# Row trips on ScalarE's DMA queue, a 256-column product placed in front of the first MLP strip, and a warm-up of five wide products in a two-block transformer kernel

## The reference

```python
h = x
a = rms_norm(h, norm_mix[i])
y = stick_breaking_mixer(a, sb_w_qkv[j], sb_w_o[j])
h = h + y
h = h + sq_relu_mlp(rms_norm(h, norm_mlp[i]), mlp_w1[i], mlp_w2[i])
return rms_norm(h, final_norm)
...
h = rms_norm_2(x, pre_mix_g[l])
z = h @ w_in[l]
```

## Time and profile before

| | us |
|---|---|
| median of 3 runs | 2128.96 |
| lowest, highest | 2128.48, 2130.49 |
| the profiled execution | 2131.68 |
| its span in the trace | 2129.9 |
| TensorE busy in it | 2117.4 |

### The profile page before, as it was taken

How to read it: one execution, slowest core, us unless ns; L and a number is a source line. 1 busy time by engine, 2 the same in 40 slices (tenths; PEclk the granted TensorE clock), 3 DMA queues, 4 the chain that set the end, 5 groups by cost and what they waited for, 6 DMA issues and landing times.

```text
span 2129.9 us, 26812 instructions
## 1 busy us (share of the span) xinstructions
PE 2117.4 (99%) x11014; PEld 1816.5 (85%) x11014; DVE 1256.3 (59%) x1337; ACT 1052.1 (49%) x1224; POOL 189.8 (9%) x90
## 2 busy tenths in 40 slices
PE   9999999999999999999999999999999999999998
PEld 8888888888888888888878888888888888888887
DVE  6554656656455554555666755475665644666565
ACT  6554555544334443444545544465555433555543
POOL 3000000000000000000004000002222100222210
PEclk9999999999999999999999999999999999999999
DMA  8565547665666666565675555555555666556663
GB/s 287 173 204 171 184 163 237 227 191 176 207 196 188 190 212 193 176 204 193 223 232 184 175 174 198 190 164 182 181 189 185 216 191 195 173 183 197 207 206 121
DMA packets 218922, 411.97 MB, mean 193 GB/s; under 512 B 13360, under 2 KB 22704, under 8 KB 218288
## 3 DMA queue, kind: packets, MB, share of 16 engines
q1 hardware_dynamic: 217936, 405.77, 59.2%
q10 hardware_dynamic: 864, 4.49, 0.6%
HBM read 403.92 MB, written 6.29 MB: 193 GB/s over the span
## 4 chain that ended last, share of the span: by engine, by line
PE 98%; DVE 0%; DMA 0%; ACT 0%; issue 0%; SPq 0%; POOL 0%; ACTq 0%; DVEq 0%; POOLq 0%
PE ps L1481 98%; DMA passed_rows<-xN 0%; PE ps L1484 0%; ACT Wh L910 0%; DMA E<-passed_rows 0%; DVE Wl L1131 0%; ACT aHL L928 0%; DVE xN L1223 0%; DVE T L1227 0%; SPq L848 0%; ACT T L922 0%; DVE xN L1214 0%; ACT T L1060 0%; DVE QK L1368 0%; ACT raw L1073 0%
## 5 line engine op out<-in xcount | busy, mean ns | idle before, releaser
L1131 DVE TENSOR_TENSOR Wl<-raw,Wh 128x1024 fp32r<-128x1024 f32 x743 | 912.1, 1246 | 649.0 <-ACT Wh L910 648.3
L1481 PE MATMUL ps<-aHL,Wh 128*128 128x512 f32 x3336 | 1162.8, 393 | 2.0 <-DVE aHL L1231 1.5
L910 ACT ACTIVATE Wh<-raw 128x1024 fp32r<-128x1024 f32 x743 | 767.5, 1054 | 587.1 <-PE ps L1481 583.3
L1481 PE MATMUL ps<-aHL,Wl 128*128 128x256 f32 x3328 | 931.9, 280 | 0.0
L1481 PEld LDWEIGHTS ps<-aHL,Wh 128*128 128x128 f32 x3336 | 625.6, 188 | 142.1 <-DVE aHL L1231 1.8
L1481 PEld LDWEIGHTS ps<-aHL,Wl 128*128 128x128 f32 x3328 | 630.6, 189 | 0.6
L1481 PE MATMUL ps<-Wh,hid 128*128 128x512 f32 x1728 | 533.2, 389 | 0.0
L1481 PEld LDWEIGHTS ps<-Wh,hid 128*128 128x128 f32 x1728 | 324.4, 188 | 67.8
L1481 PE MATMUL ps<-Wl,hid 128*128 128x512 f32 x864 | 336.4, 389 | 0.0
L1481 PEld LDWEIGHTS ps<-Wl,hid 128*128 128x128 f32 x864 | 162.2, 188 | 33.1
L1481 PE MATMUL ps<-Wh,oHL 128*128 128x512 f32 x512 | 159.0, 390 | 0.0
(11 more groups left out here) (177 smaller groups left out, 798.1 us busy)
## 6 DMA issues: line engine op xcount, KB each, us to landing
raw<-in_mlp_w_dram SPq DMA_DIRECT2D x256, 512.0 KB, 4.2
raw<-in_w_up_dram SPq DMA_DIRECT2D x176, 512.0 KB, 3.6
raw<-in_sb_w_qkv_dram SPq DMA_DIRECT2D x93, 512.0 KB, 4.7
raw<-in_w_down_dram SPq DMA_DIRECT2D x88, 512.0 KB, 4.0
raw<-in_w_in_dram SPq DMA_DIRECT2D x64, 512.0 KB, 4.3
raw<-in_sb_w_o_dram SPq DMA_DIRECT2D x32, 512.0 KB, 5.1
raw<-in_w_o_dram SPq DMA_DIRECT2D x32, 512.0 KB, 3.7
passed_rows<-xN SPq DMA_DIRECT2D x16, 256.0 KB, 4.3
```

Of the source, the lines that this page charges most:

```text
L910: e.activation(Wh[:, i % NW, :], rawv[:, i % NRAW, :], ACT.Copy).then_inc(st["hi"][0], 1)
L1131: e.tensor_tensor(Wl[:, i % NW, :], rawv[:, i % NRAW, :], Wh[:, i % NW, :].bitcast(F32), ALU.subtract).then_inc(st["lo"][0], 1)
L1481: return e.matmul(o, l, r, start=start, stop=stop, skip_group_check=True)
```

## The change

Three things are changed. The step `move_rows` is split into `pass_rows` and `return_rows`, both in ScalarE's program instead of SP's. The two passes are planned ahead of the squares of the same rows, and the four returns one piece later. The product of ones and `r_a` goes from behind the fifth piece of the first `mlp_w1` strip to in front of its first piece. The ten constant products of 128 columns at the beginning become five of 256.

```diff
--- before.py
+++ after.py
@@ -144,14 +144,11 @@
         st["r3c"], st["r4c"], st["diag"] = first["r"], both, diag
         after(p.at + 2, lambda: spread("r4", "r_b"), ahead=True)
 
-    def wide_product():
-        s = side_set()
-        step("wide_product", set=s, row=st["r1"], free=list(free[f"set{s}"]))
-
     def move_rows(n, gain_name, need):
 
-        moved = done("rows_moved", 4 * 16)
-        step("move_rows", n=n, need=need, free=list(free["E"]), passed=done("rows_passed", 32), done=moved)
+        passed, moved = done("rows_passed", 32), done("rows_moved", 4 * 16)
+        step("pass_rows", n=n, need=need, done=passed)
+        later(1, lambda: step("return_rows", n=n, passed=passed, free=list(free["E"]), done=moved))
 
         def turn_blocks():
             turned = done("blocks_turned")
@@ -270,8 +267,8 @@
             step("add_products", s4=s4, set=s, mm=k, x_rows=x_rows[-1], factor=st["r2sq"] if scaled else None, done=added)
             free[f"set{s}"] = [added[1]]
             if gain_name == "mlp":
+                move_rows(s4, "mlp", added)
                 row_squares(s4, added)
-                move_rows(s4, "mlp", added)
             if gain_name == "pre2":
                 sq = row_squares(s4, added)
 
@@ -279,8 +276,8 @@
                     g = [done("rows_gained") for t in range(2)]
                     step("gain_rows_x", n=s4, need=sq, row=st["final_row"], done=g)
                     st["final_used"] = g[1]
+                    move_rows(s4, "pre2", g)
                     row_squares(s4, g, gained=True)
-                    move_rows(s4, "pre2", g)
                 later(1, gained)
             if more:
                 more(s, k[1])
@@ -321,8 +318,7 @@
             i = strip("mlp_w1", (at + j) * STRIP, ALL8, "aHL", tile_hl, evac_relu(4 * j))
             if at + j == 0:
                 after(i + 3, lambda: row_norm(squared=True))
-                after(i + 4, wide_product)
-            elif j == 0:
+            if j == 0:
                 p.pieces[i]["wide"] = True
         for s4 in range(4):
             i = strip("mlp_w2", s4 * STRIP, tuple(range(2 * at, 2 * (at + n))), "hid1", hid_tiles,
@@ -836,17 +832,6 @@
                 elif k == "load_rows":
                     t, cs = st["c"] // 4, slice(st["c"] % 4 * STRIP, (st["c"] % 4 + 1) * STRIP)
                     e.dma_start(xN[:, t, cs], A["x_rows"][t * 128:(t + 1) * 128, cs]).then_inc(st["done"][0], 16)
-                elif k == "move_rows":
-                    n, cs = st["n"], slice(st["n"] * STRIP, (st["n"] + 1) * STRIP)
-                    for t in range(2):
-                        e.wait_ge(*st["need"][t])
-                        e.dma_start(passed[n, t * 128:(t + 1) * 128, :], xN[:, t, cs]).then_inc(st["passed"][0], 16)
-                    for t in st["free"]:
-                        e.wait_ge(*t)
-                    e.wait_ge(*st["passed"])
-                    for a in range(4):
-                        e.dma_start(moved_rows[a * 32:(a + 1) * 32, :, :],
-                                    passed[n].rearrange("(c j) (a f) -> a j c f", c=8, a=4)[a]).then_inc(st["done"][0], 16)
                 elif k == "load_half":
                     i, t = st["i"], st["t"]
                     w, _, at, col = pieces[i]["src"]
@@ -940,6 +925,18 @@
                     for t in st["need"]:
                         e.wait_ge(*t)
                     e.dma_start(dst, src).then_inc(st["done"][0], 16)
+                elif k == "pass_rows":
+                    cs = slice(st["n"] * STRIP, (st["n"] + 1) * STRIP)
+                    for t in range(2):
+                        e.wait_ge(*st["need"][t])
+                        e.dma_start(passed[st["n"], t * 128:(t + 1) * 128, :], xN[:, t, cs]).then_inc(st["done"][0], 16)
+                elif k == "return_rows":
+                    e.wait_ge(*st["passed"])
+                    for t in st["free"]:
+                        e.wait_ge(*t)
+                    for a in range(4):
+                        e.dma_start(moved_rows[a * 32:(a + 1) * 32, :, :],
+                                    passed[st["n"]].rearrange("(c j) (a f) -> a j c f", c=8, a=4)[a]).then_inc(st["done"][0], 16)
                 elif k == "norm_x":
                     cs = slice(st["q"] * STRIP, (st["q"] + 1) * STRIP)
                     for t in st["need"]:
@@ -1577,8 +1574,9 @@
                                 m.then_inc(p.mm, 1)
                 elif k == "warm_up":
                     e.wait_ge(*st["ones"])
-                    for n in range(10):
-                        mm(ps[0][:, 3, 0:128], ones[:, :], ones[:, :], True, True)
+                    for n in range(5):
+                        mm(ps[0][:, 3, 0:TOK].rearrange("p (t q) -> p t q", t=2), ones[:, :],
+                           ones[:, :].unsqueeze(1).broadcast_to([128, 2, 128]), True, True)
                 elif k == "rms":
                     P = ps[st["set"]]
                     e.wait_ge(*st["need"])
@@ -1600,11 +1598,6 @@
                             mm(ps[st["side"]][:, 0, :], diag, xn[:, 1, cs], False, True).then_inc(st["summed_out"][0], 1)
                 elif k == "turn":
                     turn_tiles(st)
-                elif k == "wide_product":
-                    for t in st["free"]:
-                        e.wait_ge(*t)
-                    e.wait_ge(*st["row"])
-                    mm(ps[st["set"]][:, 1, 0:TOK], ones[:, :], r_a[:, :], True, True)
                 elif k == "spread":
                     e.wait_ge(*st["diag"])
                     for t in st["free"]:
```

## The result

| us | before | after |
|---|---|---|
| median of 20 runs each | 2129.16 | 2133.95 |
| lowest, highest | 2127.54, 2132.55 | 2131.38, 2137.16 |
| the profiled execution | 2131.68 | 2133.41 |

The ratio is 1.0021, 95% interval [1.0015, 1.0027]. The forecast was 2129.3, in a range of 2126.5 to 2132.5: the time lies outside it, on the side to which I had given 0.08.

The account below looks back on a forecast made before the run. TensorE, busy 2117.4 of 2129.9 us, was taken as the bound. From the median 2128.96, -0.26 (product), 0 (warm-up), 0 (seven trips) and +0.6 (eighth trip) made +0.3: 2129.3 us, range 2126.5 to 2132.5.

Parts of the forecast that it names:

- the side to which I had given 0.08: Whole kernel: chance 0.08 that it becomes slower by more than 0.2%, 4.3 us.
- So seven trips cost 0: Trips behind sb_w_o and three of mlp_w2: the weights' lead covers ScalarE's stand, so 0 us.
- The 2.2 us of cover in mlp_w2: Last round of mlp_w2: weights ready at 1079.7 us, wanted at 1081.9, so a trip has 2.2 us to spare.
- the eighth trip: In front of w_in_2: +1.0 us behind Wh and Wl, -0.4 for earlier passes, together +0.6, bounds -1.3 and +3.0.
- Rival (d): ScalarE's queue starves TensorE in mlp_w2 if passes land slowly, 8.0 us: +7.0, 2136.0; chance 0.08.
- The product in front: First mlp_w1 strip: five pieces pass from 2.826 to 2.773 us, -0.26 us, bounds 0 and -0.3.
- The warm-up: Kernel start: five products of 256 end when the ten of 128 did, 0 us, bounds 0 and +0.8.
- Rival (b): First strips: the new warm-up leaves the long pace, +0.8 us, 2130.1; chance 0.10.
- the quicker 0.34 each: Eighth trip: ScalarE might issue each return in 0.34 us, 4 x 0.34 instead of 1.80, making the delay 0.8.
- The clock: Around the stall near w_in_2: 5.6 us of products at half speed lose 2.8 us, before and after alike.
- rival (a): Behind the stall at 1118 us: the pace flips from long to short, -1.6 us, 2127.7; chance 0.10.

Follow-up runs that it names:

- e8: Changed kernel with only the four returns and their wait moved back to SP's program; 2130.77 us, ratio 0.9999 to before.
- e11: e8 with ScalarE also waiting for the passes where the returns were, issuing nothing; 2130.71 us, ratio 0.9999 to before.
- e13: Changed kernel with two of the four returns issued by ScalarE and two by SP; 2130.39 us, ratio 1.0003 to before.
- e1: Kernel before with only the trips moved to ScalarE, old product and warm-up; 2130.89 us, ratio 1.0006 to before.
- e16: Changed kernel with only the mlp_w2 trips on ScalarE, those behind sb_w_o on SP; 2130.32 us, ratio 1.0001 to before.
- e5: The changed kernel run again unaltered, beside its variants on one chip; 2134.18 us, ratio 1.0015 to before.
- e15: Changed kernel with only the sb_w_o trips on ScalarE, those of mlp_w2 on SP; 2133.03 us, ratio 1.0013 to before.
- e18: Changed kernel with another product of ones and r_a in front of the second mlp_w1 strip; 2133.01 us, ratio 1.0013 to before.
- e2: Kernel before with only the 256-column product moved in front of the first mlp_w1 piece; 2129.00 us, ratio 0.9994 to before.
- e3: Kernel before with only the warm-up changed to five products of 256 columns; 2129.84 us, ratio 0.9999 to before.
- e4: e1 with the returns and their wait in SP's program, passes still on ScalarE; 2132.68 us, ratio 1.0007 to before.
- e12: Kernel before with the product in front and rel_band loaded eight pieces later; 2129.40 us, ratio 0.9996 to before.
- e17: e2 with another product of ones and r_a in front of w_in_2's third strip; 2129.77 us, ratio 0.9998 to before.
- e6: Changed kernel with the returns planned one piece later still, two behind the passes; 2145.92 us, ratio 1.0070 to before.
- e7: Changed kernel with passes and returns both in GpSimd's program; 2154.18 us, ratio 1.0109 to before.
- e9: Changed kernel with SP also waiting at the passes' place until they have landed; 2138.73 us, ratio 1.0038 to before.
- e10: e9 with SP waiting on until the returns have landed as well; 2135.95 us, ratio 1.0026 to before.
- e14: e11 with five unused copies of r_a on ScalarE where the return issues were, no DMA added; 2132.03 us, ratio 1.0011 to before.

## Why the prediction was wrong

**The step that failed** is "So seven trips cost 0". I computed the cover for one trip by itself, with the landing of 4.3 us, and compared it with the lead of the weights. For one trip this is right: behind the first, TensorE had no stall in after either. What I didn't ask is whether a late trip delays the next one. In sb_w_o it does, because the chain from one pair of passes to the next went through ScalarE and VectorE only and was 22.59 us, 0.83 over the strip. The last passes went out at 391.82, 2.8 behind the start of mlp_w1's first piece; before they went out 0.5 behind it (388.70). For these trips I had also counted the cover of the weights only, not that of the tiles of `aHL`, for which TensorE then stalled (406.9 us). The landing alone (5.5 for 4.3) doesn't do it: with 5.1 and 5.2 and the issues on SP (e8, e11), and with 5.0 and half of the issues (e13), the trips keep step. The 2.2 us of cover in mlp_w2 fell short as well, in after though not in e1 and e16.

**How much.** In the five profiles with all sb_w_o trips and returns on ScalarE and no further delay put in (after, e1, e5, e15, e18), w_in_2 begins at 1095.9 to 1097.8, on average 1096.5; in the ten with the trips on SP, or with returns there and no copies, or split (before, e2, e3, e4, e8, e11, e12, e13, e16, e17) at 1092.7 to 1094.3, on average 1093.2. (e6, e7, e9 and e10, later still, begin it at 1097.0 to 1112.4.) The difference, 3.3 of the 4.8 us, is there ahead of the eighth trip; from there to the end both groups take the same (1036.4 and 1036.2 on average). Of the 3.3, 1.3 are the long pace that three of the five (e1, e5, e15) have behind their stall, and 0.3 are the 1.4 us that only after lost in mlp_w2. By the times, e15 (+3.1) and e16 (+0.4) give 3.5 together, e5 3.8, e18 2.7, but e1 only 0.7; the intervals are some 1.8 us to each side. The rest of the 4.8 stays open.

One kernel doesn't fit as well. e14's trips are late too (its last passes go out 2.6 us behind that piece's start), but in its profile the late piece costs only 0.3 us and w_in_2 begins at 1092.7. The profile shows the cycle, and not where the 2.1 us went by which the median of e14 lies over before.

**Rival (d)** was the side that came true, but not its mechanism: it wanted a landing of over 7.3 us in the strips of mlp_w2. There a strip takes 10 x 2.72 = 27.2 us, the longest way from passes to returns in after is 6.2 us, and e16, with those trips alone on ScalarE, is at 1.0001. Its 2136.0 was nearer to 2133.95 than my forecast by accident.

**The product in front**: -0.26 forecast; e2's and e16's first round takes 133.56 us for 133.81, so -0.25. Right. In after the strip then stalls for `aHL` at 406.9 us. A gain of 0.25 in front of such a stall may only bring TensorE to it sooner; no run shows this.

**The warm-up**: 0 forecast, e3 0.9999. The five products took 4.56 us where the ten took 4.64. The first piece began at 6.20 in after, again behind its `Wl`, and the first strips went over to the long pace (2.83) at the third piece. But the pace of the first strips is not the warm-up's: with the ten old products it was short in before and e1 and long in e2, with the five new ones short in e3 and e5 and long in e8 and e9. Rival (b) fell as a mechanism; as an event it occurs with either.

**The eighth trip**: I had +1.0 for Wh and Wl, -0.4 for the landing of the passes, and nothing for that of the returns. ScalarE and VectorE there, after:

```profile
1101.70 0.93 ACTq L932 DMA_DIRECT2D passed_rows<-xN  x2
...
1107.75 1.95 ACTq L938 DMA_DIRECT2D E<-passed_rows  x4
1109.80 2.01 ACT L895 ACTIVATE Wh<-raw 128x1024 fp32r<-128x1024 f32 x2 [4.79 <-issue]
```

```profile
1110.89 2.36 DVE L1128 TENSOR_TENSOR Wl<-raw,Wh 128x1024 fp32r<-128x1024 f32 x2 [4.62 <-ACT Wh L895]
1113.23 1.25 DVE L1224 STREAM_TRANSPOSE T<-E 128x1024 f32<-128x1024 f32 x1
```

The transpose is 17.32 us behind w_in_2's start where it was 15.85: +1.5, for a forecast of +0.6. Its parts: the passes go out 1.0 later (5.79 behind that start, 4.78 before), and from there to the returns it is 1.0 less (6.05 for 7.06), so the returns begin as before, 11.84 behind the start. From there to the transpose it is 5.48, 4.01 before, so +1.5 where I had 1.0. The two `Wl` end at 1113.26, but the last return landed only at 1113.21: here both end together, and without the `Wl` the transpose would have been hardly sooner. In e16 the `Wl` decide, 1.3 us behind the last landing; in e8 and e11, with the returns on SP, the transpose waits for the returns alone and comes 19.0 and 18.6 behind the start. So the price that I named was there, and beside it one of the same size that I had at nothing, the later landing of the returns. The four issues take 1.95, not the quicker 0.34 each that I half believed.

I had read the Trainium skill ("DMA: Bandwidth & Descriptors", "Issuing engines are not separate DMA queues") as saying that the landing would not move. It says that transfers started by different engines run on the same 16 DMA engines and interleave. The landing moved: over the whole span the passes took 5.5 us for 4.3 and the returns 3.5 for 2.6, with SP's loads running on beside them. In e16, which has this eighth trip, the transpose is 18.3 behind the start and the whole is +0.4 with an interval of some 1.8 to each side, so no later end could be told from the times.

**The clock**: I kept the loss of 2.8 us on both sides. It isn't kept. Around the fall in after, and in e2:

```profile
1115.28:1122.11 6.83, 5.46 (x16) 4.30 (x16) 5.36 (x23) 3.72 (x8) 0.00 (x0) 0.52 0.48 150
```

```profile
1112.98:1116.39 3.41, 3.41 (x12) 2.93 (x12) 2.50 (x11) 0.83 (x2) 0.00 (x0) 0.52 0.32 85
```

In after the piece at half speed (1.2 GHz) ran while the diagonal was being made, and the 3.2 us of waiting for it became 0.7: nothing was lost. In before the spread's product itself came at half speed, and the pieces behind it too. From the spread's product to the end of the span it is 1012.0 us in before and 1009.5 in after; the difference is as large as the 2.5 us by which the profile of before lies over its median. The fall lasted 6.83 us in after and 3.41 in e5, the same kernel, and with the trips on SP 6.83 in before and 3.41 in e2 and e3. So the difference isn't shown to be the change's.

**The pace behind that stop**, rival (a): long in 14 of the 20 profiles, short in e4, e8, e10, e14, e16 and e17, wherever the trips are. Nothing shows that the change flips it.

## What to carry to other kernels

When a blocking step is moved into an engine's program, don't compare its delay with the slack once: follow the chain from this occurrence to the next one, and if it closes without passing through the engine that paces the kernel, its length must be under the period. The trips at 27.2 us per strip cost nothing that the times could show when they were moved alone (though one profile had a stall of 0.93 us there), those at 21.76 cost some 3 us, and 1 us less on ScalarE, two issues given to SP, took most of it away. The stand by itself and the slower landing by itself cost nothing that could be measured. And an estimate of cover must include what the moved wait makes slower: here the landing of the returns, which I had left as it was.

## What the runs showed of the hardware that I had not expected

The pace of equal products (16 per piece) is 2.773 or 2.827 us, and it usually holds for a whole stretch. Behind a stop it can come out either way with the same code: 41 pieces in 113.70 us in after, in 115.90 in e5. In other places it is always the same: the first five pieces of w_in_2 are at the long one in all 20 profiles. What sets it stays open.

The granted clock falls to 1.2 GHz for 3.41, 6.83 or (in e6) 10.24 us at varying moments around the same stall, and costs from 0 to 2.5 us, by whether TensorE has other waiting to do. Both make single executions of one kernel differ by more than some parts of this change cost, so a span of one profile couldn't judge it.
